# Score units between the blocks of the value projection, in layer 0 of a four-layer hybrid diffusion block

## The reference, cut to what matters

```
def gqa_mixer(h_lat, h_ctx, w_qkv, q_norm, k_norm, w_o, cos, sin, with_ctx_out):
    ...
    q_l = apply_rope(rms_norm(q_l, q_norm), cos, sin)
    k_l = apply_rope(k_l, cos, sin)
    k_all = jnp.concatenate([k_c, k_l], axis=2)
    v_all = jnp.concatenate([v_c, v_l], axis=2)
    def attend(q, k, v):
        s = jnp.einsum("bkgqd,bkld->bkgql", q, k).astype(jnp.float32) * scale
        p = _softmax32(s).astype(v.dtype)
        return jnp.einsum("bkgql,bkld->bkgqd", p, v)
```

## Time and profile before

| what | us |
|---|---|
| median of 3 runs (2392.67 to 2394.89) | 2394.16 |
| time of the profiled execution | 2390.34 |
| its span, first to last instruction | 2388.5 |
| values and attention of layer 0, from the squares of the last tile to the last PV (115.53 to 212.86) | 97.3 |
| TensorE busy over the span | 2320.3 |
| VectorE busy over the span | 1736.1 |
| ScalarE busy over the span | 1127.2 |

### The profile page before, as it was taken

How to read it: one execution, slowest core, us unless ns; L and a number is a source line. 1 busy time by engine, 2 the same in 40 slices (tenths; PEclk the granted TensorE clock), 3 DMA queues, 4 the chain that set the end, 5 groups by cost and what they waited for, 6 DMA issues and landing times.

```text
span 2388.5 us, 35814 instructions
## 1 busy us (share of the span) xinstructions
PE 2320.3 (97%) x13842; PEld 1896.4 (79%) x13842; DVE 1736.1 (73%) x2667; ACT 1127.2 (47%) x1946; POOL 335.9 (14%) x269
## 2 busy tenths in 40 slices
PE   7999999999999899999999998899999999999998
PEld 5655988887988468888879777788888889848998
DVE  3685799987575977999865237778999835487874
ACT  3575643433432766434324444455443325286663
POOL 0000411111200013111112004331111111002110
PEclk9999999999999999999999999999999999999999
DMA  9603555556233032555553320044555635404664
GB/s 317 203 19 95 171 167 159 165 157 191 87 97 97 10 112 76 169 165 161 179 155 88 107 80 28 2 150 125 165 152 164 200 95 132 129 10 135 183 183 127
DMA packets 449965, 310.88 MB, mean 130 GB/s; under 512 B 11954, under 2 KB 405858, under 8 KB 449540
## 3 DMA queue, kind: packets, MB, share of 16 engines
q1 hardware_dynamic: 447024, 307.03, 43.7%
q10 hardware_dynamic: 2772, 1.56, 0.2%
HBM read 307.50 MB, written 1.05 MB: 129 GB/s over the span
## 4 chain that ended last, share of the span: by engine, by line
PE 86%; DVE 6%; ACT 4%; issue 2%; SPq 1%; DMA 1%; ACTq 0%; DVEq 0%
PE bank L1734 75%; PE bank L2050 1%; PE bank L2070 1%; DVE stat L1344 1%; PE bank L2114 1%; ACT p L824 1%; DVE q_part L1403 1%; PE bank L1819 1%; DVE slab_lo L1074 1%; PE bank L1799 1%; ACT pt L836 1%; ACT hb L641 1%; ACT slab_hi L624 1%; PE bank L1811 0%; PE bank L2165 0%
## 5 line engine op out<-in xcount | busy, mean ns | idle before, releaser
L1734 PE MATMUL bank<-h_hi,slab_hi 128*128 128x512 f32 (+1 forms) x2416 | 840.4, 348 | 7.2 <-ACT slab_hi L624 3.8
L1734 PE MATMUL bank<-h_lo,slab_hi 128*128 128x512 f32 (+1 forms) x2416 | 829.1, 343 | 0.0
L1734 PE MATMUL bank<-h_hi,slab_lo 128*128 128x512 f32 (+1 forms) x2416 | 828.7, 343 | 0.0
L1074 DVE TENSOR_TENSOR slab_lo<-slab_raw,slab_hi 128x1024 fp32r<-128x1024 f32 (+1 forms) x388 | 526.7, 1358 | 257.9 <-ACT slab_hi L624 256.5
L624 ACT ACTIVATE slab_hi<-slab_raw 128x1024 fp32r<-128x1024 f32 (+1 forms) x388 | 401.0, 1035 | 285.1 <-PE bank L1734 225.4
L1734 PEld LDWEIGHTS bank<-h_hi,slab_hi 128*128 128x128 f32 x2416 | 458.1, 190 | 90.0 <-issue 25.2
L1734 PEld LDWEIGHTS bank<-h_hi,slab_lo 128*128 128x128 f32 x2416 | 458.2, 190 | 53.9
L1734 PEld LDWEIGHTS bank<-h_lo,slab_hi 128*128 128x128 f32 x2416 | 458.4, 190 | 53.0 <-issue 1.0
L1048 ACT ACTIVATE conv<-bank,prm 128x512 f32<-128x512 f32 (+1 forms) x176 | 127.9, 727 | 447.0 <-PE bank L1734 447.0
L1099 DVE SCALAR_TENSOR_TENSOR mod_sum<-slab_raw,cond_wide,mod_sum 128x512 f32<-128x512 f32 x420 | 316.7, 812 | 0.1
L1734 PE MATMUL bank<-g_hi,slab_hi 128*128 128x512 f32 (+1 forms) x788 | 272.8, 346 | 0.0
(11 more groups left out here) (253 smaller groups left out, 2658.7 us busy)
## 6 DMA issues: line engine op xcount, KB each, us to landing
slab_raw<-in_ffn_w_up SPq DMA_DIRECT2D x176, 512.0 KB, 3.9
slab_raw<-in_mod_w SPq DMA_DIRECT2D x132, 512.0 KB, 4.5
slab_raw<-in_ffn_w_down SPq DMA_DIRECT2D x64, 512.0 KB, 3.7
slab_open<-in_mod_w SPq DMA_DIRECT2D x36, 512.0 KB, 7.3
slab_gap<-in_mod_w SPq DMA_DIRECT2D x24, 512.0 KB, 8.1
slab_raw<-in_ffn_w_down SPq DMA_DIRECT2D x32, 384.0 KB, 3.2
slab_raw<-in_b_w_qkv SPq DMA_DIRECT2D x24, 512.0 KB, 3.7
slab_raw<-in_c_w_in SPq DMA_DIRECT2D x24, 512.0 KB, 3.8
```

The source lines that it names most:

```text
L1074: nc.vector.tensor_tensor(wlo[slot][:, 0:w], raw[of][:, 0:w], whi[slot][:, 0:w].bitcast(f32), ALU.subtract).then_inc(s_lo, 1)
L1734: ins = mm(out, l, r, start=first and n == 0, stop=last and n == 2, skip_group_check=parted)
```

## The change

In layer 0 the value blocks go to banks 5 and 6, so banks 0 to 3 are free for scores as soon as the norms 6 to 9 have read them. PE then runs: value block 0, squares of tile 9, value block 1, scores of units 0 and 1, `mod_turn(1)`, value block 2, scores of units 2 and 3, value block 3, and the rest of the attention.

DVE runs: norm 8, the copy of the modulation rows, norm 9, rotary part 7, attention steps 0 to 3, `mod_evacuate`, the two value copies, steps 4 to 7, rotary part 8, steps 8 to 11, rotary part 9, steps 12 to 15, splits 13 and 14, and the rest. ACT runs its steps 0 to 15 right behind the root of tile 9, then its splits 13 and 14, and the rest. Two waits are new on PE (`bank_cleared` for the first four scores; the transpose of unit 1 waits for the first value copy), and two waits for free banks before the value blocks go. The other layers keep their order.

```
+EARLY = (0,)
...
                 roots(9)
+                attention(0, 0, 16)
                 for q in range(2):
                     split(n + AHEAD)
...
-            def attention(i):
+            def attention(i, first, last=None):
...
-                                          bank[(fg + half) % 4][:].rearrange("p (t c) -> p t c", t=2)
+                                          bank[5 + half][:].rearrange("p (t c) -> p t c", t=2)
...
-                    if ft >= 2:
+                    if 2 <= ft < 9:
                         rope(S, ft - 2, rope_t, (s_free["dve"], freed[fg + ft - 2][1]))
                 mod_row_copy(1)
                 norm(9)
+                rope(S, 7, rope_t, (s_free["dve"], freed[fg + 7][1]))
+                attention(0, 0, 4)
+                mod_evacuate(0, 4, 9, 1)
+                values(n, fg + 10)
+                attention(0, 4, 8)
                 rope(S, 8, rope_t, (s_free["dve"], freed[fg + 8][1]))
+                attention(0, 8, 12)
                 rope(S, 9, rope_t, (s_free["dve"], freed[fg + 9][1]))
+                attention(0, 12, 16)
                 splits_to(n + 1 + AHEAD)
-                values(n, fg + 10)
-                mod_evacuate(0, 4, 9, 1)
...
-            def v_project(n, fg):
+            def v_project(n, *tts):
                 split_ready(n + 1)
-                for tt in range(4):
-                    if tt % 2 == 0:
-                        group_free(fg + tt // 2)
-                    out = bank[(fg + tt // 2) % 4][:, 256 * (tt % 2):256 * (tt % 2) + 256]
+                for tt in tts:
+                    out = bank[5 + tt // 2][:, 256 * (tt % 2):256 * (tt % 2) + 256]
...
+                v_project(n, 0)
                 squares(9)
-                v_project(n, fg + 10)
+                v_project(n, 1)
+                attention(0, -1, 0)
                 mod_turn(1)
+                v_project(n, 2)
+                attention(0, 0, 2)
+                v_project(n, 3)
...
+                def bank_cleared(b):
+                    at = start["wo", i][1] - (3 if i == 0 else 5)
+                    pe.wait_ge(s_free["dve"], freed[at - (at - b) % 4][1])
+                early = i in EARLY
...
                         if maps * u + m < 4:
-                            values_copied(maps * u + m)
+                            (bank_cleared if early else values_copied)(maps * u + m)
...
+                        if early and w < 2 and (i or w):
+                            pe.wait_ge(s_free["dve"], freed[start["wo", i][1] - (4 - w if i else 2)][1])
...
-                gla() if i == 2 else attention(i)
+                gla() if i == 2 else attention(i, (2, -1, None, -1)[i])
```

More of the change, by code:

```diff
@@ L808, in copy_context @@
                                              ACT.Copy).then_inc(S["context_copied"], 1)
-                if i == 3:
+                if i == 3 and first == 0:
                     copy_context(0)
-                for u in range(len(U) + TURN + 10):
+                for u in range(first, len(U) + TURN + 10 if last is None else last):
                     if u < len(U):
@@ L1028, in _ @@
                     qkv_plain(i, n, fg)
-                gla(start["qkv", 2][0] + 16) if i == 2 else attention(i)
+                gla(start["qkv", 2][0] + 16) if i == 2 else attention(i, (16, 0, None, 0)[i])
                 n, fg = start["wo", i]
@@ L2020, in attention @@
                 c = slice(CTX, T) if i == 3 else slice(0, T)
-                if i == 3:
+                if i == 3 and first < 0:
                     pe.wait_ge(s_free["act"], freed[start["wo", i][1] - 9][1])
-                elif i == 1:
+                elif i == 1 and first < 0:
                     pe.wait_ge(S["qk_ready"], 16)
-                else:
+                elif first < 0:
                     pe.wait_ge(s_kd, 4)
                 def values_copied(b):
-                    last = start["wo", i][1] - 1
-                    pe.wait_ge(s_free["dve"], freed[last - (last - b) % 4][1])
+                    at = start["wo", i][1] - 1
+                    pe.wait_ge(s_free["dve"], freed[at - (at - b) % 4][1])
+                def bank_cleared(b):
+                    at = start["wo", i][1] - (3 if i == 0 else 5)
+                    pe.wait_ge(s_free["dve"], freed[at - (at - b) % 4][1])
+                early = i in EARLY
                 def score(u):
@@ L2056, in turn_free @@
                         pe.wait_ge(S["rs_ready"], before[1] + 1)
-                for u in range(-1, len(U) + TURN + 6):
+                for u in range(first, len(U) + TURN + 6 if last is None else last):
                     if maps == 1 and u % 2:
```

## The result

The changed kernel takes 2398.06 us (median of 17 runs, 2393.41 to 2403.25), the kernel before 2392.3 (17 runs, 2390.46 to 2396.59). The ratio is 1.0022, interval 1.0015 to 1.0029: with 2392.3 that is 5.3 us slower, 3.6 to 6.9. The forecast was 5.0 slower.

The account below looks back on a forecast made before the run. PE was taken to bound the kernel (86% of the chain ending last). A delay of 3.5 us at unit 15 plus 1.5 for the clock gave 5.0 slower, added to the median 2394.16: 2399.2 us, range 2395.3 to 2402.5.

Parts of the forecast that it names:

- The start: Start of layer 0's attention: PE's 1.53 us wait goes, reduce of unit 4 and first PV come 3.6 us earlier.
- What stands in its way: Units 4 to 16: moved rotary parts and splits spend the 3.6 us gain and delay the transpose of unit 15 by 3.5.
- It stays: Behind the transpose of unit 15: PE is busiest and hands back nothing, so the 3.5 us delay remains.
- The clock: Behind PE's wait at unit 15: granted clock falls to 0.50, costing 1.5 us more, bounds 0 and 1.7.
- dearer: Rival: an earlier wait at unit 7 also lowers the clock, or the fall lasts twice as long; +7, 2401.2 us, chance 0.14.
- The clock stays: Rival: no clock fall behind the wait at unit 15, wait paid once; +3.5, 2397.7 us, chance 0.20.
- Absorbed: Rival: DVE and ACT reach unit 16 in time, PE keeps its head start; -3.6, 2390.6 us, chance 0.07.
- Half absorbed: Rival: units 4 to 15 run some 2 us tighter, wait under 2 us, clock stays; +1.5, 2395.7 us, chance 0.09.
- At nothing: Items costed at zero: delayed loads, `mod_evacuate` ahead of the copies, waits for cleared banks and value copies, rotary parts 8 and 9.
- The sum: Whole kernel: 3.5 for the delay plus 1.5 for the clock, 5.0 us slower, 2399.2 us; chance 0.50.

Follow-up runs that it names:

- e7: Changed kernel with ACT's copy-out of unit 13 ahead of its exponential of unit 16; 2398.86 us, +5.5 us against the kernel before.
- e1: Changed kernel with splits 13 and 14 moved back ahead of or early in the attention, rotary parts as changed; 2393.59 us, +1.4 against the kernel before.
- e2: Changed kernel with 8 and 15 useless matmuls in PE's waits before the transposes of units 7 and 15; 2399.12 us, +6.9 against the kernel before.
- e4: Changed kernel with both splits and rotary parts 7 to 9 moved into DVE's pauses; 2388.70 us, -3.6 against the kernel before.
- e6: Changed kernel with only 4 and 7 useless matmuls before the transposes of units 7 and 15; 2397.78 us, +4.3 against the kernel before.
- e3: Changed kernel with rotary parts 7 to 9 moved back ahead of unit 2, splits as changed; 2394.76 us, +2.2 against the kernel before.
- e8: Changed kernel again, unedited, for a second trace and timing; 2398.18 us, +4.8 against the kernel before.
- e5: Changed kernel with the new order on PE and banks only, DVE and ACT in their old order; 2393.22 us, +0.5 against the kernel before.

## Why the prediction was right, point by point

**The start.** Right. Aligned, the first scores came at 120.52 (forecast 120.6), the value copies at 128.92 (128.7), the first PV at 134.91 (134.7), the reduce of unit 4 at 130.13 (129.9). Against the old 133.50 the gain is 3.4; 3.6 was forecast. The missing 0.2 comes in with the value copies and stays in every later term.

**What stands in its way.** Right, with the same 0.2 to 0.3 throughout: reduces of units 8, 12, 14 and 16 at 137.42, 143.54, 145.91 and 152.65, forecast 137.1, 143.3, 145.65 and 152.4. The splits on ACT started at 149.25 (149.0), those on DVE at 150.37 (150.1). Copy-out 13 ended at 154.21 and the transpose of unit 15 started at 154.36, where 153.9 was forecast; of the 0.46, some 0.3 is that lag and 0.15 the step from the copy-out to the transpose, which the prediction read (0.17) but did not add. So the term of +3.5 measures +3.95, +3.99 and +3.83. That it was the copy-out was right but not the whole of it: the division of unit 15 on DVE, 0.5 earlier, holds the same place, as e7 shows. The prediction walked past that second link; it costs nothing in the sum, but is what a repair would meet.

**It stays.** Right. From T15 to the output projection, e1, e2, e4 and e6, with a full clock there, add -0.06 to +0.12: the delay at unit 15 arrives whole. That the moved work cannot hide in pauses holds for this order alone. The prediction set two pauses of 1.5 against that work, and named the idle time before 128.7 only beside a rival: DVE stood idle for 2.38 ahead of norm 9 and for 1.77 ahead of unit 2, and e4 puts rotary part 7 and split 13 there.

**The clock.** Right in kind, and in size for the second trace: 1.55 behind T15, where 1.5 was taken; e3 and e7 give 1.57 and 1.60. In the first trace it was 2.57, the longer fall that stood among the rivals as dearer. The fall behind the wait at unit 7, which that rival feared as well, came in both traces and was all but free. The Trainium skill ("TensorE: Matmul & The Clock Gate", section "What's actually happening") says of the clock's rise at a kernel's start that its moment varies from run to run, as the hardware's watch on activity does not start with the kernel. The traces show the like for falls in the middle: the same code lost 5.12 and 3.41 us here, and a wait of 1.9 at unit 7 was followed by a fall in two traces of the changed kernel and in e7, and by none in e1.

**The rivals.** "The clock stays" did not happen in the two traces of the changed kernel. "Absorbed" is what e4 makes true by another placement: its mechanism was right and its price of 3.6 about right (3.25 in the trace, 3.6 by the times). Its condition, the reduce of unit 16 by 148.8, was met there (145.30, counted from the same squares) and not by the change, where that reduce came at 152.65. With the splits back (e1) or the rotary parts back (e3) the attention costs +0.9 or, the clock aside, +0.35: either group alone uses up the gain and a little more, both together overdraw it. "Half absorbed" did not come.

**At nothing.** The loads were hidden: the two issued at 152.34 and 153.47 fill slots that work behind 219.97 reads, and PE waits for no load in the attention. They came some 2 us later than the "about 150" of the prediction, as a slot is free only when DVE has made its half too. A price for going in and out of the value blocks did not show beyond the 0.2 above.

**The sum.** 3.5 + 1.5 = 5.0 forecast; 3.99 + 1.55 = 5.54 in one trace, 3.95 + 2.57 = 6.52 in the other, +5.3 and +4.8 by the times. The times alone do not hold up the second term: 3.9, with no price of the clock, lies in their intervals too, and it is the traces that show it. That 5.0 stands so near the median is in part luck, as the first term was 0.3 to 0.5 short in the traces, and the second between 0.05 and 1.1. How often the longer fall comes is open: two traces are no count, and the mean of 2.9 us over the runs of e8 only says that two short falls are nearer the rule than the 5.12 of the first trace.

## What to carry to other kernels

Starting a chain of work earlier is worth its head start only down to the first place where another engine is late; find that place by walking the new order through the timelines of all engines, and count what was moved in front of it. A wait that appears in a profile is a delay only by as much as the instruction behind it starts later than before, so compare that start, counted from a common point upstream. Where a moved operation has to wait its turn somewhere, look for an engine's own pauses in the old timeline and cut the operation to fit them.

## What the runs showed of the hardware beyond that

The granted clock's falls come in portions: over the ten traces each fall from 112 us on, but for those that the kernel's end cuts short, lacked 1.71 or 3.41 us of full speed, to 0.01. Behind the attention, from 220 to 2380, the traces lack between 5.1 and 10.2 us, in three to five such falls. They lie at a few places in code that is the same: near 790 and near 1460 in every trace, near 1475, 1510, 1535 and 2105 in some. Which of these fall, and by which portion, differs from trace to trace.

That is as much as this whole change, and explains part of why runs of one kernel spread over some 6 to 10 us here: over the 33 runs of the kernel before beside e5 to e8, the mean granted clock and the time correlate at -0.54. The rest of the spread is open.

A fall in a stretch where PE waits for another engine anyway cost at most 0.16 us here; the same fall in a stretch where PE sets the pace costs 1.55 to 1.60 of its 1.71.
